# A hybrid encoder layer with a mixture of experts: sums and logits spread between TensorE's large products, and four edits around them

## The reference

```python
h = rms_norm(x, g_mix); z = h @ w_in                       # 1024 -> 1536
y_conv = silu(layer_norm(conv31(c_val * sigmoid(c_gate)))) # 512 channels, causal
y = gelu(s5_scan(s_in))                                    # 512 channels, 64 complex states a group
y_ssm = y * sigmoid(y @ glu_w + glu_b)
x = x + concat(rms_norm(y_conv), rms_norm(y_ssm)) @ w_out  # each of the two with its own norm
h = rms_norm(x, g_ffn)
logits = h @ w_router + b_router                           # 4 groups + 32 experts
# group top-1, expert top-2 in it, gates; assignments sorted by expert in blocks of 128
x = x + sum over the two experts of gate * ((silu(h @ w_gate) * (h @ w_up)) @ w_down)
out = rms_norm(x, g_final)
```

## Time and profile before

| | us |
|---|---|
| median of 3 runs | 1811.09 |
| lowest, highest | 1805.53, 1813.3 |
| profiled execution, its own time | 1799.83 |
| its span | 1798.4 |

### The profile page before, as it was taken

One profiled execution on the slowest core, in us unless ns is written; L12 is line 12 of the kernel. 1 busy time (PEld: TensorE's weight loads), 2 busy tenths in 40 slices (PEclk: granted clock), 3 DMA queues, 4 the chain that ended last, 5 costly groups with the idle time before them and its releaser, 6 DMA issues.

```text
span 1798.4 us, 32269 instructions
## 1 busy us (share of the span) xinstructions
PE 1609.5 (89%) x11107; PEld 1481.7 (82%) x11108; DVE 1126.1 (63%) x1688; ACT 825.0 (46%) x1024; POOL 618.4 (34%) x887
## 2 busy tenths in 40 slices
PE   6999999599937999999379999999999999999990
PEld 6989899588836888887278999999999999999980
DVE  6766655365447567665446747654765888665666
ACT  3412211136354333342325646654665786655563
POOL 0777767444243226554321222222222221212120
PEclk9999999799968999999579999999999999999995
DMA  8723342598463224322459878886888999888878
GB/s 278 228 103 126 118 154 85 160 276 255 144 220 112 94 94 141 105 72 94 165 199 327 294 243 285 272 318 198 282 265 271 385 401 388 294 259 286 284 244 340
DMA packets 125699, 398.23 MB, mean 221 GB/s; under 512 B 33214, under 2 KB 60224, under 8 KB 98624
## 3 DMA queue, kind: packets, MB, share of 16 engines
q1 hardware_dynamic: 101712, 329.97, 50.3%
q0 software_dynamic: 20224, 58.87, 13.4%
q10 hardware_dynamic: 3696, 8.50, 1.3%
HBM read 311.30 MB, written 85.99 MB: 221 GB/s over the span
## 4 chain that ended last, share of the span: by engine, by line
PE 42%; DMA 4%; DVE 3%; issue 1%; ACT 1%; POOL 0%; DVEq 0%; SPq 0%; ACTq 0%; POOLq 0%
PE moe_p_y L2249 4%; PE moe_p_y L2252 4%; PE moe_p_y L2250 4%; PE moe_p_g0u L2234 4%; PE moe_p_g0u L2236 4%; PE moe_p_g0u L2235 4%; PE moe_p_x L2226 2%; PE moe_p_u L2236 2%; PE moe_p_g L2236 2%; PE moe_p_u L2235 2%; PE moe_p_g L2234 2%; PE moe_p_g L2235 2%; PE moe_p_u L2234 2%; DMA residual<-moe_y,moe_ids_s 2%; PE moe_p_hid L2242 1%
## 5 line engine op out<-in xcount | busy, mean ns | idle before, releaser
L1714 DVE TENSOR_TENSOR expert_lo<-expert_raw,expert_hi 128x2048 fp32r<-128x2048 f32 x192 | 432.9, 2284 | 58.2 <-ACT expert_hi L1710 50.2
L1710 ACT CAST expert_hi<-expert_raw 128x2048 fp32r<-128x2048 f32 x192 | 362.0, 1912 | 15.3 <-PE moe_p_u L2236 7.9
L706 PE MATMUL proj_p_z<-proj_x_hi,proj_w_hi 128*128 128x256 f32 x768 | 223.5, 291 | 14.2 <-DVE proj_x_lo L554 14.2
L707 PE MATMUL proj_p_z<-proj_x_lo,proj_w_hi 128*128 128x256 f32 x768 | 219.2, 285 | 0.0
L708 PE MATMUL proj_p_z<-proj_x_hi,proj_w_lo 128*128 128x256 f32 x768 | 219.1, 285 | 0.0
L2234 PE MATMUL moe_p_g0u<-expert_hi,moe_xh 128*128 128x256 f32 x736 | 211.2, 287 | 1.5 <-DVE moe_xl L2107 1.5
L2235 PE MATMUL moe_p_g0u<-expert_hi,moe_xl 128*128 128x256 f32 x736 | 207.2, 281 | 0.0
L2236 PE MATMUL moe_p_g0u<-expert_lo,moe_xh 128*128 128x256 f32 x736 | 207.1, 281 | 0.0
L706 PEld LDWEIGHTS proj_p_z<-proj_x_hi,proj_w_hi 128*128 128x128 f32 x768 | 149.2, 194 | 20.9 <-issue 19.8
L1997 POOL DMA_INDIRECT residual<-moe_y,moe_ids_s x45 | 76.5, 1699 | 232.8 <-ACT moe_y L2038 227.6
L2249 PE MATMUL moe_p_y<-expert_hi,moe_hh 128*128 128x512 f32 x368 | 153.4, 417 | 0.0
(11 more groups left out here) (429 smaller groups left out, 4141.6 us busy)
## 6 DMA issues: line engine op xcount, KB each, us to landing
expert_raw<-in_experts SPq DMA_DIRECT2D x192, 1024.0 KB, 8.3
ffn_input<-mix_h SPq DMA_DIRECT2D x17, 512.0 KB, 4.0
proj_x_sb<-in_x SPq DMA_DIRECT2D x8, 1024.0 KB, 8.5
turns<-proj_turn POOLq DMA_DIRECT2D x16, 512.0 KB, 4.5
cs_tw<-turns SPq DMA_DIRECT2D x16, 512.0 KB, 8.0
mix_x_sb<-in_x SPq DMA_DIRECT2D x16, 512.0 KB, 5.2
residual<-mix_x SPq DMA_DIRECT2D x16, 512.0 KB, 2.7
proj_x_raw<-in_x_turned SPq DMA_DIRECT2D x7, 1024.0 KB, 6.2
```

Source lines behind the costliest of these rows:

```text
L706: nc.tensor.matmul(o, whi, x_hi[:, half, c], start=start, stop=False)
L707: nc.tensor.matmul(o, whi, x_lo[:, half, c], start=False, stop=False)
L1710: self.nc.scalar.copy(self.hi[:, u], self.raw[:, u]).then_inc(self.hi_done, 1)
L1714: tensor_tensor(self.lo[:, u], self.raw[:, u], self.hi[:, u].bitcast(FP32), ALU.subtract).then_inc(self.lo_done, 1)
```

## The change

It has five parts.

1. `convolution_and_ssm`: ACT finishes the last tile one slot earlier, ahead of the last two `copy_y`. Three semaphores of cleared edges become one.
2. `mix`, step 0: DVE halves the gate's bias (`half_glb`) behind the statistics and not ahead of them. The splits of the output weights are placed otherwise: ACT's pieces 3 and 4 ahead of the Silus, DVE's pieces 3 and 4 with 2, and 5 and 6 between `cat_lo`, `ys` and the second `cat_lo`.
3. `mix`, steps 1 to 8: the sums stand one by one behind the first four groups of three products of `out_tile(2n-2)`, the logits of tile 2n-4 behind eight later groups of the same tile, the logits of tile 2n-3 behind eight groups of the gate product (in step 8 behind groups of the second tile). The rows of `h` are still turned where they were, but nothing waits behind them; `ln_in`, `ln_out` and `glu` wait for ACT's copies where they need a bank. Even tiles are turned into `pa` first. DVE reads the logits where its list has them now: tile 2n-4 behind the four additions of tile 2n-2, tile 2n-3 behind the first `cat_lo`, and the choice behind that.
4. `experts`, last routing: slots first, then gates. POOL scatters token numbers alone (eight scatters), loads and gathers the first block, and scatters the gates (eight more) in between, all before the first load of `ids_s`. DVE splits two weight pieces ahead of `turn_x(0)` and four behind.
5. `experts`: SP loads the second expert's pieces only when the first gather has landed.

```diff
@@ convolution_and_ssm, ACT
-                if tile_ending(m - 2) is not None:
-                    finish(tile_ending(m - 2))
+                for t in range(CT):
+                    if finished_in(t) == m:
+                        finish(t)
+        def finished_in(t):
+            ends = [m for m in range(SLOTS) if tile_ending(m) == t][0]
+            return ends + (1 if t == CT - 1 else 2)
@@ mix, ACT
+        def turned_banks(q):
+            return (pc, pa) if q % 2 else (pa, pc)
                 if first(n):
                     conv_part(n, par)
-                    split_hi(range(3, 5))
+                    split_hi(range(5, 6))
                     gate_part(n)
-                    split_hi(range(5, 7))
+                    split_hi(range(6, 7))
                     ssm_part(n, par)
@@ mix, DVE
-            dve.wait_ge(cols_in, 32)
-            V.tensor_scalar(half_glb[:, :], cols[:, GLB, :], 0.5, None, ALU.mult).then_inc(ln_scale, 1)
                 if first(n):
                     statistics(n)
+                    dve.wait_ge(cols_in, 32)
+                    V.tensor_scalar(half_glb[:, :], cols[:, GLB, :], 0.5, None, ALU.mult).then_inc(ln_scale, 1)
                     gelu_argument(n)
                     split_lo(range(0, 2))
                     gelu(n)
-                    split_lo(range(2, 3))
+                    split_lo(range(2, 5))
...
                 if not first(n):
-                    out_tile(n * 2 - 2, n - 1, 0)
-                    if not (isinstance(n, int) and n == 1):
-                        logit(n * 2 - 3, 1)
+                    out_tile(n * 2 - 2, n - 1, 0, between=lambda: logit(n * 2 - 4, 0) if n > 1 else None)
+                if last_step(n):
+                    logit(n * 2 - 3, 1)
...
+                def while_gated(k):
+                    if k == 0 and n > 1:
+                        logit(n * 2 - 3, 1)
+                        if chosen_in(n):
+                            choose((n - 3) // 2)
+
                 if first(n):
-                    split_lo(range(3, 7))
-                if not last_step(n):
-                    front2(n, par)
-                if first(n):
+                    front2(n, par, lambda k: split_lo(range(5 + k, 6 + k)))
                     split_lo(range(7, PIECES))
+                elif not last_step(n):
+                    front2(n, par, while_gated)
                 if not first(n):
-
-                    out_tile(n * 2 - 1, n - 1, 1, between=lambda: logit(n * 2 - 2, 0))
+                    out_tile(n * 2 - 1, n - 1, 1, between=lambda: logit(n * 2 - 2, 0) if last_step(n) else None)
@@ mix, TensorE
+            OF_FIRST = (5, 6, 8, 9, 10, 11, 12, 13)
+            OF_GATE = (2, 3, 4, 5, 6, 8, 9, 10)
+                def beside_first(i):
+                    if i < 4:
+                        sums(n - 1, i)
+                    elif i in OF_FIRST and n > 1:
+                        logit(n * 2 - 4, OF_FIRST.index(i), n)
+                def beside_gate(i):
+                    if i in OF_GATE and n > 1:
+                        logit(n * 2 - 3, OF_GATE.index(i), n)
                 if not first(n):
-                    sums(n - 1)
-                    out_tile(n * 2 - 2, n - 1, 0, 1 - par)
-                    if not (isinstance(n, int) and n == 1):
+                    out_tile(n * 2 - 2, n - 1, 0, 1 - par, beside_first)
+                    if n > 1:
                         if not last_step(n):
                             pe.wait_ge(yn_done, n + 1)
-                        logit(n * 2 - 3, 1, n)
+                        turn_tile(n * 2 - 3, 1)
                 if not last_step(n):
                     ln_out(n)
-                    glu(n)
+                    glu(n, beside_gate)
@@ experts
+            sp.wait_ge(x_in, 16)
...
-            for i in range(FIRST, TT):
-                for k in range(2):
-                    routing.scatter(nc.gpsimd, scratch["table"], i, k).then_inc(scattered_last, 16)
+            for n in range(2 * LT):
+                scatter(0, n, scattered_last)
             pool.wait_ge(scattered_last, 16 * 2 * LT)
             load_ids(0)
             gather(0)
+            pool.wait_ge(routed, GATED)
+            for n in range(0, 2):
+                scatter(1, n, gates_last)
             pool.wait_ge(routed, COUNTED)
...
             dve.wait_ge(scattered_last, 16 * 2 * LT)
-            for u in range(weights.PIECES):
+            for u in (G0, U0):
                 weights.split_lo(dve, V.tensor_tensor, 0, u)
             turn_x(0)
+            for u in (G1, U1, D0, D1):
+                weights.split_lo(dve, V.tensor_tensor, 0, u)
```

More of the change, by code:

```diff
@@ L1288, in place @@
                 tiles = slice(LT * m, LT * m + LT)
-                choice.slots(G, step, pick[:, :], rank[:, :], routing.slot_i[:, tiles])
+                slots = choice.slots(G, step, pick[:, :], rank[:, :])
+                step(G.tensor_copy(routing.slot_i[:, tiles], slots))
                 choice.gates(G, step, chosen_exps[:, :], recip[:, :], routing.pay[:, tiles])
@@ L1836, in exponentials, with slots @@
         step(E.tensor_tensor(den, den, self.psum[:, :], ALU.mult))
-    def slots(self, E, step, pick, rank, slot_i):
+    def slots(self, E, step, pick, rank):
         T = self.T
@@ L1955, in load_ids @@
             def load_ids(row):
-                pool.dma_start(ids_g[:, :], table[row]).then_inc(ids_g_in, 16)
+                with nc.allow_non_contiguous_dma(reason="the tokens' numbers without the gates"):
+                    pool.dma_start(ids_g[:, 0:1], table[row][:, 0:1]).then_inc(ids_g_in, 16)
             def row_of(b):
```

137 lines of the change are left out of this document (88 added, 49 removed).

## The result

The changed kernel takes 1845.28 us (median of 4 runs, 1840.07 to 1849.08), the kernel before 1808.31 (4 runs, 1805.52 to 1813.3): ratio 1.0205, 95% interval 1.0177 to 1.0232. It is 2% slower, where 0.25% slower was predicted, and lies outside the range.

What follows compares the result with a forecast made beforehand. The mixing stage was taken as bound, only just, by TensorE. Terms -3.6 - 7.4 + 17.0 + 3 - 4.5 = +4.5 us on 1799.8 (+0.25%), applied to the median 1811.1, gave 1815 us, range 1794 to 1833.

Steps and rivals of the forecast that it cites:

- The convolution's last tile: End of the convolution: ACT's earlier finish brings the barrier ahead of mixing forward, -3.6 us, bounds -2 to -5.
- Step 0: Mixing's step 0: half_glb behind the statistics and moved weight pieces bring POOL's squares earlier, -7.4 us, bounds -4 to -9.
- Streaming: Mixing steps on TensorE: a spread logit pair costs 0.22 us, so spreading saves nothing; bounds -3.6 to +1.8 a step.
- Waits: Mixing steps: three new TensorE waits of 2.5, 2.2 and 2.0 us lengthen the stage from 297.2 to 314.2, +17.0 us.
- The clock: Mixing steps: two added short falls to half clock, 1.7 us lost in each, +3 us, bounds 0 and +20.
- the slower rival: Mixing steps: clock falls at the new waits, behind the turned-back rows each step, +15 to +20 more, 1832 us; 28%.
- The experts' start: Last routing to first expert product: earlier scatters and a faster first gather, -4.5 us, bounds 0 and -6.5.
- The last early choice: Step 8 to the barrier into the experts: no term in the sum, listed as predicted 0.
- Signs: Wrong if the period stays under 41 us or half clock exceeds 30 in steps 2 to 8; first rows turned near 900.
- The faster rival's price: Mixing steps: the loop over engines doesn't bind, step about 36.5 us, stage 297, total -15, 1796 us; 22%.

Runs made afterwards that it cites:

- fill: The changed kernel plus products with unused results where TensorE would stand, at three places in each of steps 2 to 7; 1818.12 us, ratio 1.0034.
- cast_only: The changed kernel with ACT casting yg before it copies the turned rows; 1801.76 us, ratio 0.9959 to the kernel before.
- three_out: The changed kernel with the first tile's logits later, yg cast before the turned rows' copy, and odd tiles' logits in another bank; 1785.09 us, ratio 0.9847.
- recip_early: three_out with DVE's reciprocal for the last early choice put ahead of its read of logits 13 in step 8; 1778.06 us, ratio 0.9837.
- grouped: recip_early with the 16 pieces of each logits in one group inside the first tile or the gate product, not as pairs; 1763.86 us, ratio 0.9759.
- group_at_wait: The changed kernel, its three waits kept, with the 16 pieces of each logits in one group where the first pair stood; 1849.85 us, ratio 1.0214.
- bank_only: The changed kernel with the odd tile's logits gathered in a bank of their own; 1821.77 us, ratio 1.0071 to the kernel before.
- late_only: The changed kernel with the first tile's logits behind groups 8 to 14 instead of 5 to 13; 1826.83 us, ratio 1.0109.

## Why the prediction was wrong

**The sign was right, and so were the new waits; the clock's term was not, and three smaller terms were off.** Of the 40.8 us between +4.5 and +45.3, 26 are the clock, 6.6 the experts, 4.6 the barrier into them (a term that the sum did not have), 3.0 step 0, 2 the waits, less 1.5 for the convolution's end.

- **The convolution's last tile** (-3.6): the barrier came at 500.5, -5.1, at the bound. Where mixing starts varies, though: its first turning lies between 501.1 and 510.6 us in the kernels that have this part, at 509.3 and 515.2 in the two that don't.
- **Step 0** (-7.4): -4.4, near the bound of -4. DVE's half_glb did leave the chain. But the prediction counted only the pieces that leave ACT's chain: two pieces of the output weights (2.19 us) now stand ahead of the Silus, and the convolution's half of cat_hi is made 25.4 us behind the barrier (525.88) and not 23.9 (529.50 before). POOL's last square is released 8.9 us earlier, 5.1 of them from the barrier:

```profile
541.27 0.37 PE L1640 MATMUL mix_pd<-mix_ones,mix_sq 128*128 128x1 f32 x1 [1.14 <-POOL mix_sq L1318]
```

- **Streaming**: right. A pair costs 0.22 us between 512-column products (a period of 0.92 less 3 x 0.233) and 0.23 in the gate product, the value taken from the turned pair, far from 0.04. By the Trainium skill's page "TensorE: Matmul & The Clock Gate", section "Step-by-step: what each phase is for", loads are pulled ahead of matmuls in flight; in this trace the pair costs 0.22 us all the same.
- **Waits** (+17.0): right. 2.4, 2.0 and 1.8 us in step 5 against 2.5, 2.2 and 2.0; after a choice 3.1 to 3.2 against 3.8. The third is shorter, down to 0.8 us, where the clock had fallen already. At full clock the stage is 316.2 us (fill), forecast 314.2.
- **The clock** (+3): this is the step that failed: "I add two falls as short as the shorter ones, 1.7 us lost in each". There are ten falls of 3.4 to 13.7 us, and they cost 29 us: the stage takes 345.5, and 316.2 with the waits filled and no fall. It was the slower rival, given 28%, in the place that it named, behind the turned-back rows in each step. Four more stood at the first wait, where the rival counted the large products on both sides against a fall. But its price too, 15 to 20 us more, was some 8 short. Two things spoke for it: before, the clock fell behind 0.9 us of standing, and I was about to add waits of 2 to 3. I let the one row without a fall, at 709.30, stand against them. The Trainium skill's page "TensorE: Matmul & The Clock Gate", section "Part 4: PE-mode transpose", says transposes don't count as busy for the clock. By it the clock would have fallen in every step, as it did; that it is the turned rows was not shown: in cast_only and three_out the same rows are turned without a wait behind them, and no fall begins there.
- **The experts' start** (-4.5): -3.8 up to the first product, with the first gather 5.7 us from issue to turned rows where I took 5.4. What I left out is that SP's held-back loads then run into the second gather, which TensorE waits for (view of waits, 951 to 1000):

```profile
PE moe_p_x L2308 <- DMA moe_xg<-ffn_input,moe_ids_g: 2.4, 1, 2.4
```

  I had charged the second block with POOL's late ids at 1 us, not with this. A second wait, 2.2 us for DVE's `moe_hid`, comes ahead of the fifth block; no run takes it apart. Up to that block's turned rows, 5.6 of the +5.9 us are lost.
- **The last early choice** (0): not in the sum at all. The reciprocal stood one logits read further back in step 8, so POOL's eight scatters came later, and the barrier behind them by 4.6 us (recip_early takes this back). It is a moved instruction whose waiters I did not follow to their end.
- **Signs.** Period over 41 us and half clock over 30 us in the steps: the text had named the second as what would make it wrong. The first block's rows, said to come near 900, were turned at 948.2. The steps' loss hides the gain there, but the sign did not fit the prediction's own sum either: 908.86 with its terms is some 912.
- **The faster rival's price.** It was worked wrongly. With a step of 36.5 us the prediction's own sum gives a stage of about 270 us and not 297, and a time near 1770 and not 1796. grouped, with periods of 36.7 and 37.6, has a stage of 272.1 us and takes 1763.9. So the room that a better order had was some 27 us larger than the text said.

## What to carry to other kernels

A wait placed inside a loop is not worth only its length: here some 36 us of standing cost another 29 through the clock. So ask of each new wait what the clock did in the same trace behind shorter ones, and give it that price. To use work as cover, put it where its inputs have long been ready, late in a tile; whether it is spread or in one piece matters much less than when its first piece is asked for. When an instruction moves, follow its waiters on the quiet engines too (here POOL's scatters) up to the next barrier.

## What the runs showed of the hardware

- Work without use can shorten a kernel: 308 products of 256 columns in the waits took some 27 us off.
- A fall, once begun, lasted 3.4 to 13.7 us at 1.2 GHz although TensorE was busy nearly throughout (12.31 of 13.65 us in the window at 697.30), whether small pieces were spread among the products (the changed kernel) or stood in one group (group_at_wait, 3.4 to 10.2 us).
- Standing of 2.0 us behind 16 turned pieces was followed by a fall in three of six steps of bank_only; the 16 turned pieces with no wait behind them by none in cast_only, three_out and grouped.
- The barrier into the experts came 6.8 to 9.8 us behind the end of POOL's last scatter instruction in the eight kernels in which it came over 4 us behind the last logits: 916.4 against 909.6 in the changed kernel, 859.3 against 850.7 in three_out, 900.0 against 890.2 in late_only.
- DVE beside POOL: in step 0 of the changed kernel the `cat_lo` that runs beside POOL's cubes took 2.68 us; the one at 752.59, with POOL idle, took 1.22. The one at 537.18, beside POOL's first addition of squares, took 1.23, and there it was POOL's instruction that took 2.32 us, against 1.30 in step 5 (764.81).
